# Order of the expert weight loads in a two-layer hybrid MoE encoder: gate and up of expert e+2 ahead of down of expert e+1

## The reference, cut to what matters

```python
h = rms_norm(x, ffn_norm_w[i])
x = x + hier_moe(h, router_w_group[i], router_b_group[i], router_w_expert[i],
                 router_b_expert[i], exp_w_gate[i], exp_w_up[i], exp_w_down[i])
# inside hier_moe, for a block of an expert's tokens:
hid = jax.nn.silu(xblk @ w_gate[e]) * (xblk @ w_up[e])
return hid @ w_down[e]
```

## Time and profile before

| | |
|---|---|
| time, median of 3 runs | 2976.38 us (2976.2 to 2980.21) |
| span of the profiled execution | 2971.0 us |
| tensor engine busy (matmul) | 2421.0 us, 81% |
| vector engine busy | 787.3 us, 26% |
| scalar engine busy | 640.3 us, 22% |
| GpSimd busy | 514.2 us, 17% |
| bytes moved | 701.12 MB, mean 236 GB/s |
| expert weights among them | 384 loads of 1.5 MiB, on SP's queue |

### The profile page before, as it was taken

One profiled execution on the slowest core, in us unless ns is written; L12 is line 12 of the kernel. 1 busy time (PEld: TensorE's weight loads), 2 busy tenths in 40 slices (PEclk: granted clock), 3 DMA queues, 4 the chain that ended last, 5 costly groups with the idle time before them and its releaser, 6 DMA issues. The chain is left out here.

```text
span 2971.0 us, 35580 instructions
## 1 busy us (share of the span) xinstructions
PE 2421.0 (81%) x11822; PEld 1434.1 (48%) x11822; DVE 787.3 (26%) x2377; ACT 640.3 (22%) x1328; POOL 514.2 (17%) x775
## 2 busy tenths in 40 slices
PE   7999877778878777758699999989587788787773
PEld 5888663333333333335588888768233333333331
DVE  4222650000000000050666666526200000000003
ACT  3111211111001101131255555542001111001011
POOL 2121312111111111110111111021111111111110
PEclk9999988899898988969899999999789998989897
DMA  4112037999999999950000000101799999999997
GB/s 118 43 43 85 29 156 293 390 372 390 383 388 386 395 381 390 383 187 0 8 8 9 8 15 0 57 15 73 279 381 380 395 384 383 389 383 392 382 386 298
DMA packets 202294, 701.12 MB, mean 236 GB/s; under 512 B 36192, under 2 KB 65888, under 8 KB 202224
## 3 DMA queue, kind: packets, MB, share of 16 engines
q1 hardware_dynamic: 181744, 666.65, 56.7%
q0 software_dynamic: 20480, 33.64, 3.0%
HBM read 687.59 MB, written 46.14 MB: 247 GB/s over the span
## 5 line engine op out<-in xcount | busy, mean ns | idle before, releaser
L1230 PE MATMUL ps<-arena 128*64 128x384 f32 x4096 | 822.4, 563 | 326.3 <-DMA arena<-in_exp_w_up 323.9
L1230 PEld LDWEIGHTS ps<-arena 128*64 128x64 f32 x4096 | 327.2, 158 | 765.6 <-issue 714.5
L1133 DVE TENSOR_TENSOR arena<-ps,xw 128x512 f32<-128x512 f32 x128 | 88.5, 691 | 1122.2 <-PE ps L1220 1122.2
L1249 PE MATMUL ps<-arena 128*64 128x512 f32 x1536 | 357.7, 600 | 2.2 <-DVE arena L1142 2.2
L1040 ACT ACTIVATE arena<-ps 128x384 f32<-128x384 f32 x128 | 62.9, 491 | 1086.2 <-PE ps L1230 1086.2
L815 PE MATMUL ps<-hT_split,w_split 128*128 128x512 f32 x1152 | 264.5, 391 | 3.1 <-DVE hT_split L291 3.1
L815 PEld LDWEIGHTS ps<-hT_split,w_split 128*128 128x128 f32 x1152 | 217.0, 189 | 49.0 <-DVE hT_split L291 3.9
L996 POOL COPY col_idx<-scatter_idx 128x1 int32 (+1 forms) x128 | 23.4, 182 | 1104.1 <-ACT arena L1051 1104.1
L1249 PEld LDWEIGHTS ps<-arena 128*64 128x64 f32 x1536 | 99.3, 136 | 164.3 <-issue 149.3
L1051 ACT ACTIVATE arena<-ps 128x512 f32<-128x512 f32 x128 | 76.4, 597 | 372.4 <-PE ps L1249 372.4
L989 POOL DMA_INDIRECT arena<-h_rows,col_idx x128 | 134.5, 1051 | 115.3 <-POOL col_idx L986 108.3
(11 more groups left out here) (201 smaller groups left out, 2783.2 us busy)
## 6 DMA issues: line engine op xcount, KB each, us to landing
arena<-in_exp_w_gate SPq DMA_DIRECT2D x128, 1536.0 KB, 11.2
arena<-in_exp_w_up SPq DMA_DIRECT2D x128, 1536.0 KB, 14.4
arena<-in_exp_w_down SPq DMA_DIRECT2D x128, 1536.0 KB, 8.3
arena<-y_rows SPq DMA_DIRECT2D x16, 1024.0 KB, 10.9
arena<-in_conv_w_in SPq DMA_DIRECT2D x24, 512.0 KB, 3.6
h_rows<-rows SPq DMA_DIRECT2D x16, 512.0 KB, 2.6
x<-in_x SPq DMA_DIRECT2D x8, 512.0 KB, 7.5
arena<-in_conv_w_out SPq DMA_DIRECT2D x2, 2048.0 KB, 9.9
```

The costliest lines, as they stand in the source:

```text
L1133: dve.tensor_tensor(xT[:, slot, :, :, :].rearrange("p j h m -> p (j h) m"), c.ps[:, slot, :].rearrange("p (a m) -> p a m", m=RANKS), bc(c. ...
L1230: last_ = pe.matmul(c.ps[row:row + RANKS, 2 + slot, 0:FF], xT[:, slot, j, half, :], w[:, slot, half, j * FF:(j + 1) * FF], start=(half + j ...
L1249: last_ = pe.matmul(c.ps[half * RANKS:(half + 1) * RANKS, 6 + slot, :], hidden[:, slot, j, :], w_down[:, slot, j, half * BANK:(half + 1) * ...
```

## The change

In `moe_phase`, SP's loop now issues gate and up of expert g + 2 as soon as gate and up of g have been multiplied, and then down of g + 1 as soon as down of g - 1 has. The order in the queue becomes gate and up of 2, down of 1, gate and up of 3, down of 2, and so on; the down of expert 63 is issued behind the loop. The loads that the phase before issues are now gate and up of 0, the row store, gate and up of 1, down of 0; the down of 1 is left to the loop's first step. Buffers, bytes, number of DMAs and the other engines' programs are as they were.

```diff
@@ -443,9 +443,8 @@
         sp.wait_ge(self.products, 2 * NT)
         self.experts.load_gate_up(sp, 0, 0)
         self.norm.sp_store(sp, NT - 1)
+        self.experts.load_gate_up(sp, 1, 1)
         self.experts.load_down(sp, 0, 0)
-        self.experts.load_gate_up(sp, 1, 1)
-        self.experts.load_down(sp, 1, 1)
         for t in range(4):
             sp.wait_ge(self.norm.rows_stored[t], 16 * NT // 4)
 
@@ -947,14 +946,15 @@
         @block.sync
         def _(sp):
             count = rounds(sp)
-            with sp.Fori(1, count * (NE // 2)) as pair:
+            with sp.Fori(0, count * (NE // 2) - 1) as pair:
                 g = pair * 2
                 for slot in range(2):
-                    e = (g + slot) % NE
-                    sp.wait_ge(gate_up_products, g + slot + free(0))
-                    experts.load_gate_up(sp, slot, e)
-                    sp.wait_ge(y_products, g + slot + free(0))
-                    experts.load_down(sp, slot, e)
+                    sp.wait_ge(gate_up_products, g + slot + done(0))
+                    experts.load_gate_up(sp, slot, (g + slot + 2) % NE)
+                    sp.wait_ge(y_products, g + slot + free(1))
+                    experts.load_down(sp, 1 - slot, (g + slot + 1) % NE)
+            sp.wait_ge(y_products, count * NE)
+            experts.load_down(sp, 1, NE - 1)
 
             sp.wait_ge(y_stored, count * NE + AHEAD)
             for t in range(NT):
```

## The result

The changed kernel takes 2858.2 us (median of 4 runs, 2857.12 to 2863.36), against 2976.3 us before; the ratio is 0.9625 with a 95% interval from 0.9597 to 0.9652. The profiled execution has a span of 2855.9 us, 115.1 less than before. The forecast was 2853.5 us and 122.9 us less. In the sets run later the kernel before has medians near 2970 us, so the gain in time is 111 to 118 us. One execution of the kernel before, in the second later set, took 3965.65 us at a granted clock of 0.556 and is left out of its median.

What follows compares the result with a forecast made beforehand. Bound: expert loads, with the queue running dry once every two experts. With pauses gone, 307.3 MB per layer at 418 GB/s saves 61.8 and 61.1 us, 122.9 together: span 2848.1 plus 5.4 gives 2853.5 us, range 2834 to 2892.

Steps and rivals of the forecast that it cites:

- The part that gives the gain: Expert phases: gate and up of e + 2 issued right after the product gate and up of e, ending the queue's pauses.
- Cover: Queued loads outlast the time from a landing to the next first byte: 15.1 us against 11.6 at worst, 3.5 us left.
- no stretch of 2 us under 350 GB/s: Sign expected in the profile after, between the first and the last load, if the prediction was right.
- The rate: Queue speed in the expert phases: 418 GB/s taken, 408 to 423 possible, giving 2889 to 2836 us.
- Down's load: Down of e + 1, queued behind gate and up of e + 2, lands before its product needs it, 1.6 us to spare.
- Starts and ends: Phase edges: down of 1 adds 1.57 MB to the path, down of 62 takes 1.57 MB off; net nothing.
- The rival that the engine would alternate between its two levels: Expert phases: the tensor engine at its lower clock becomes the bound, 11.89 us per expert, 2861 us; chance 0.06.
- The ceiling: Rival in the load queue: steady work falls back to the mean 388 GB/s, time stays 2976 us; chance 0.04.
- the half pause: Rival at SP's issue into a full queue: half the holes remain, 61 of 123 us, 2915 us; chance 0.05.
- the slower case: Rival: the queue shares itself among loads, so the product down waits for its load, 3021 us; chance 0.05.

## Why the prediction was right, and where it was off

**What bounds the kernel.** Right, and shown: the loads, with a pause in every second expert. The pause's cause, the chain from landing to issue against what is queued, is shown by the two kernels with shorter products and by the one with a third buffer; its size is only roughly that of the sum.

**The part that gives the gain.** The prediction put it down to both the moment of the issue and the 6.29 MB queued behind a landing, and named the part after the moment ("gate and up of e + 2 right after the product"). The runs say that the second half of that argument carries it: 2860.7 us with the late issue and the new order.

**Cover.** I cost the pause at nothing, with 3.5 us of cover at worst. The sum behind that is wrong by half a us: 8.3 + 1.3 + 0.5 + 2 is 12.1 and not 11.6, which leaves 3.0 of the 15.1; it also leaves out the indirect DMAs, which it had counted in the 11.9 us of the old order. Early in a phase the cost of nothing held: 422 GB/s over 80 us without a hole. Later it did not quite, and the sign "no stretch of 2 us under 350 GB/s" failed, with 14 such stretches, the deepest at 147. They cost little, as the rates over the whole phases are 417 and 416.

**The rate.** This is the term that was mis-sized. The sum has 418 GB/s; counted by landings, 4.981 MB in 12.02 us, it is 414, with 422 moved at a phase's start and 411 late. That makes 0.10 us an expert, 6 us a layer. For layer 0 the sum said 1199.3 and the trace says 1206.06, 6.8 us more. By an estimate 0.7 of them are the first issue, at 461.51 and not 460.83. About 2 are 307.3 MB at 417 in place of 418. The other 4 are the two late parts, since at the end of the phase the last of a gate and up lands about 4 us behind the other parts, and the queue has moved bytes of later loads meanwhile. The three stretches of 20 us on which I based the rate lay right behind a pause each, in a kernel in which the spread is small.

**What luck there was.** The two phases miss by 6.8 us each. The span misses by 7.8 only (122.9 forecast, 115.1 measured), because the time behind each phase's last gate and up, which I had left as it was, became 2.5 and 3.3 us shorter. Part of that is that product itself, 7.07 and 5.38 us in place of 8.29 and 8.16. And the forecast of the time, 2853.5, starts from a median of 2976.38 for the kernel before; from the 2968.8 of the next set the same 122.9 us less would be 2845.9, against 2858.0 measured there.

**Down's load.** Right: no wait for it, at 1.6 us of reckoned slack.

**Starts and ends.** "Net nothing" was half right. Keeping down of 1 early makes the phases 2 to 3 us shorter in the one execution profiled, so the changed kernel may leave a little on the table; the times do not show it beyond their noise.

**Clock.** The rival that the engine would alternate between its two levels came true in kind: nearly every second product takes about 7.1 us (three in layer 0 take 8.3 to 8.4), behind a wait of 2.4 to 3.2 us, the others 5.38, and the mean granted clock rose from 0.911 to 0.927. It costs nothing that shows, as the chain with a product of 7.1 us, 9.19 + 7.08 - 5.38 = 10.9 us, stays below the period of the loads. A wait of 2.58 us ahead of 508.45 left the clock at full, one of 2.40 ahead of 520.11 did not, so these waits alone do not tell which of the two comes.

**The other rivals.** The ceiling fell with 422 GB/s over 80 us and 417 over 724 us; the half pause and the slower case did not come.

## What to carry to other kernels

With two buffers of each operand, put the loads in the queue in the order in which their buffers come free; then count as a first, rough guide, at the moment a load lands, the bytes still queued behind it against the time from that landing to the next load's first byte, with the consumer at its slow clock. A queue that pauses shows as stretches of 2 us below the plateau at the same place in every period, and only such short stretches show it: the mean of 388 GB/s looked like a limit and was none. Where the queue then runs nearly without a pause, expect a little less than the rate of the stretches between pauses, and more so late in a long phase.

## What the runs showed of the hardware

The 16 parts of a load are not served alike when gathers and scatters from GpSimd run beside it. Within 16 experts (some 190 us) they drift apart by 7 us, and late in the phase the drift lies in two of the sixteen, up to 5.7 us behind the other fourteen in layer 0 and 6.8 in layer 1. Without any indirect DMA the spread stays at 1.6 us (the last two parts 1.3 behind) and the rate at 424 GB/s; with gathers alone or scatters alone the drift is there, slower, at 417 to 424 GB/s. In the kernel before, which pauses some 2 us in every 26, the spread is 0.5 and 1.3 us in the median of down's two buffers, so its profile hardly shows the drift. The Trainium skill, DMA: Bandwidth & Descriptors, section "Latency and other measured facts", says that two of the 16 DMA engines are usually slower and suspects the descriptor rings of the GpSimd path. The trace agrees that two parts lag, and that the lag grows only beside the indirect DMAs. With one kind alone the two stand out less in layer 0, 1.5 to 2.7 us behind the others at the end; in layer 1 it is up to 4.4 without the gathers. The landing records don't name the engine, and no run here tells whether the rings are the reason.

What stays open: whether the indirect DMAs slow the two parts by their descriptors or by their data, how the drift lowers the rate, and how to spread the loads' bytes so that the two get less. It wasn't tried.
